# The front of a two-block transformer kernel: weights laid out by the host in one-transfer units, modulation columns by pairs of k-tiles, and a new order of norms, splits and decays

## The reference, cut to what matters

```
s_lat, s_ctx = silu(c), silu(c_ctx)
shift, scale, ... = split(s @ ada_w[i] + ada_b[i], 6)       # for latent and context
h = rms_norm(x) * (1 + scale) + shift                        # for x and for ctx
q, k, v, g = split(h @ ret_w_in)                             # retention, 4 heads; 1024 + 1024 + 2048 + 2048 columns
log_gamma = log_sigmoid(ret_decay_logit)                     # the decays of the retention masks
```

## Time and profile before

| | us |
|---|---|
| median of 3 runs | 2016.64 (2016.51 to 2016.98) |
| the profiled execution, its own time | 2016.68 |
| its span, first to last instruction | 2014.9 |
| TensorE busy in the span | 1981.0 |
| VectorE, ScalarE busy | 1323.6, 850.2 |
| mean granted TensorE clock | 0.997 of full |

### The profile page before, as it was taken

The page is one execution under the profiler, slowest core; times in us unless marked ns, Lnnn a source line. Parts: engine busy times, 40 slices in busy tenths (PEclk is TensorE's granted clock), DMA queues, the critical chain, the costliest instruction groups (busy, mean ns, idle before and its releaser), DMA issues.

```text
span 2014.9 us, 25505 instructions
## 1 busy us (share of the span) xinstructions
PE 1981.0 (98%) x10295; PEld 1650.7 (82%) x10295; DVE 1323.6 (66%) x1610; ACT 850.2 (42%) x1003; POOL 69.0 (3%) x122
## 2 busy tenths in 40 slices
PE   8999999999999999999999999999999999999998
PEld 6878778778888888877778888898888888988887
DVE  4887978556544354677676565766866577678565
ACT  4332332124222222446665553554544356545442
POOL 0000000000111001000000000000000000000000
PEclk9999999999999999999999999999999999999999
DMA  9644444243554243332136565544665555546552
GB/s 355 203 137 138 146 160 148 76 160 90 162 167 158 89 150 132 105 105 84 63 110 206 174 180 182 187 161 168 209 201 194 170 172 163 195 161 216 190 190 80
DMA packets 250807, 319.32 MB, mean 158 GB/s; under 512 B 10129, under 2 KB 166082, under 8 KB 250178
## 3 DMA queue, kind: packets, MB, share of 16 engines
q1 hardware_dynamic: 235152, 262.77, 40.4%
q0 software_dynamic: 14464, 53.27, 7.8%
q10 hardware_dynamic: 1074, 1.66, 0.2%
HBM read 316.61 MB, written 1.05 MB: 158 GB/s over the span
## 4 chain that ended last, share of the span: by engine, by line
PE 86%; DVE 6%; DVEq 2%; ACT 2%; DMA 1%; issue 1%; ACTq 1%; SPq 0%
PE ps L2325 13%; PE ps L2326 12%; PE ps L2320 6%; PE ps L2890 6%; PE ps L3151 6%; PE ps L2339 5%; PE ps L2335 5%; PE ps L2336 5%; PE ps L2807 3%; PE ps L2268 3%; PE ps L3154 3%; PE ps L2420 2%; PE ps L2896 2%; PE ps L2900 2%; PE ps L2897 2%; PE ps L2810 2%
## 5 line engine op out<-in xcount | busy, mean ns | idle before, releaser
L1244 DVE TENSOR_TENSOR w_lo<-raw,w_hi 128x2048 fp32r<-128x2048 f32 (+1 forms) x244 | 552.9, 2271 | 224.7 <-ACT w_hi L614 224.0
L614 ACT ACTIVATE w_hi<-raw 128x2048 fp32r<-128x2048 f32 (+1 forms) x244 | 462.0, 1898 | 291.5 <-PE ps L2320 185.9
L2325 PE MATMUL ps<-w_hi,big_hi 128*128 128x512 f32 x760 | 298.6, 393 | 0.8 <-DVE big_lo L1738 0.5
L2326 PE MATMUL ps<-w_hi,big_lo 128*128 128x512 f32 x760 | 296.1, 390 | 0.0
L2335 PE MATMUL ps<-hT_hi,w_hi 128*128 128x512 f32 (+1 forms) x512 | 192.2, 380 | 1.9 <-issue 1.0
L2336 PE MATMUL ps<-hT_lo,w_hi 128*128 128x512 f32 (+1 forms) x512 | 190.2, 376 | 0.0
L2325 PEld LDWEIGHTS ps<-w_hi,big_hi 128*128 128x128 f32 x760 | 142.8, 188 | 30.3 <-issue 1.0
L2326 PEld LDWEIGHTS ps<-w_hi,big_lo 128*128 128x128 f32 x760 | 142.8, 188 | 29.0 <-issue 0.5
L3151 PE MATMUL ps<-h_both,w_hi 128*128 128x512 f32 x512 | 127.9, 392 | 0.0
L1366 DVE SCALAR_TENSOR_TENSOR raw<-front,const,raw 128x512 f32<-128x512 f32 x168 | 118.8, 748 | 7.1 <-issue 1.3
L2339 PE MATMUL ps<-hT_hi,w_lo 128*128 128x512 f32 (+1 forms) x512 | 119.8, 376 | 0.6 <-DVE w_lo L1244 0.6
(11 more groups left out here) (320 smaller groups left out, 3151.1 us busy)
## 6 DMA issues: line engine op xcount, KB each, us to landing
raw<-ffn_w_in SPq DMA_DIRECT2D x88, 512.0 KB, 5.2
raw<-w_in SPq DMA_DIRECT2D x80, 512.0 KB, 4.6
raw<-w_up SPq DMA_DIRECT2D x64, 512.0 KB, 4.7
raw<-w_down SPq DMA_DIRECT2D x64, 512.0 KB, 4.5
raw<-ret_w_in SPq DMA_DIRECT2D x48, 512.0 KB, 5.4
front<-ada_w POOLq DMA_DIRECT2D x24, 1024.0 KB, 5.5
raw<-ffn_w_out SPq DMA_DIRECT2D x40, 512.0 KB, 4.3
raw<-ada_w POOLq DMA_DIRECT2D x64, 256.0 KB, 4.2
```

The source lines that it names most:

```text
L614: act.activation(SPLIT_HI[PAIR_OF[u]][:, 0:m], raw[:, RAW_OF[u], 0:m], ACT.Copy).then_inc(sem["hi_ready"], 1)
L1244: op(SPLIT_LO[PAIR_OF[u]][:, 0:m], raw[:, RAW_OF[u], 0:m], SPLIT_HI[PAIR_OF[u]][:, 0:m].bitcast(F32), ALU.subtract).then_inc(sem["lo_ready ...
L2325: pe.matmul(out, x[0][:, t * P:(t + 1) * P], w, start=start, stop=False)
L2326: pe.matmul(out, x[1][:, t * P:(t + 1) * P], w, start=False, stop=False)
```

## The change

- **Units.** The host lays every unit out as it stands in `raw` (`units`, 8 KiB per partition in one piece), in order of use, and SP issues one DMA for each. The matrices `ada_w` are laid out the same way (`ada`). The two-DMA code of SP is gone; the waits for `lo_ready` stay.
- **Modulation chunks.** Chunk j now has the shift and the scale columns of k-tiles 2j and 2j + 1 (256 + 256 columns), so that two k-tiles of both are complete after each chunk. ACT copies the sums (`row`), DVE's `mod_cols` makes two reductions and two additions and signals.
- **Shift and scale** of layer 0's first norm are applied by DVE (`modulated`: two operations on 256 columns, the split in high and low on 512), one k-tile at a time, latent and context together.
- **Columns** and the identity come in one DMA of ACT, already as columns; the transposes of the small vectors, their copies and the separate identity load are gone.
- **Orders.** SP: x, ctx, qa0, chunks 0, 1, 2, qb0, chunk 3, g00 and the rest. POOL fetches the tables after chunk 2 is summed, and its first pieces of further chunks after chunk 3. ACT: both norms, four turned tiles, then copies and splits in turn, g00's high part before head 0 begins. DVE: both norms, then `mod_cols`, `modulated` and the splits in turn, g00's low part and `decay_end` before head 0 begins. TensorE: qa0 and qb0 with 512 columns, a k-tile at a time, and more `awake` matmuls (128 columns, 24 at the start, 4 + 4 + 8 later).
- DVE's list for head 0 is otherwise the same, with one more wait, for the rotation tables.

The core of the diff (`weight_units`, not shown, yields the same slices in the same order as SP's old code; `modulation(2)` and `(3)` keep their places around `load(FIRST_END["qb0"])`):

```diff
-        const = sb("const", [P, C_HELD])
-        cols = sb("cols", [P, 161])
+        held = sb("held", [P, 161 + C_HELD])
+        cols, const = held[:, 0:161], held[:, 161:161 + C_HELD]
...
+            def load(n):
+
+                while s.loaded < n:
+                    u = s.loaded
+                    r, v, m = RAW_OF[u], RAW_BEFORE[u], SIZES[u]
+                    if v is not None:
+                        sp.wait_ge(sem["lo_ready"], v + 1)
+                    sp.dma_start(raw[:, r, 0:m], A["units"][u, :, 0:m]).then_inc(unit_in[r], 16)
+                    s.loaded += 1
...
+                for h in range(2):
+                    sp.dma_start(FRONT_IN[2 * j + h], A["ada"][j, :, 4 * h:4 * h + 4, :]).then_inc(front_in[2 * j + h], 16)
...
             sp.dma_start(X4[:, 0:2, :], token_rows(A["x"][0])).then_inc(sem["x_in"], 16)
+            sp.dma_start(X4[:, 2:4, :], token_rows(A["ctx"][0])).then_inc(sem["xc_in"], 16)
+            load(FIRST_END["qa0"])
             modulation(0)
-            sp.dma_start(FRONT_IN[3][:, 2:4, :], kpn(A["ada_w"][0])[:, 6:8, FRONT[1] * 512:(FRONT[1] + 1) * 512]).then_inc(front_in[3], 16)
-            part(w, 0, 0, RH * RDK)
+            modulation(1)
...
+            load(TOTAL_UNITS)
...
-            pool.wait_ge(front_in[3], 32)
-            fetch(X4[:, 2:4, :], token_rows(A["ctx"][0]), sem["xc_in"])
-            pool.wait_ge(sem["front_used"], 2)
             fetch(dec[:, 0, :], bcast(A["ret_decay_logit"].rearrange("a b c -> a (b c)"), 8), sem["dec_in"])
...
+            pool.wait_ge(sem["front_used"], 3)
+            fetch(const[:, C_DIST:C_SZ], A["table"][:, C_DIST:C_SZ], sem["const_in"])
+            fetch(const[:, C_RS:C_SEL], A["table"][:, C_RS:C_SEL], sem["rot_in"])
+            fetch(ROT_COS[1], A["table"][:, C_RK:C_RK + 256], sem["rot_in"])
             pool.wait_ge(sem["front_used"], 4)
-            fetch(const[:, C_DIST:C_SZ], A["table"][:, C_DIST:C_SZ], sem["const_in"])
-            fetch(const[:, C_RS:C_SEL], A["table"][:, C_RS:C_SEL], sem["const_in"])
-            pool.wait_ge(sem["mod_ready"], 4)
-            fetch(ROT_COS[1], A["table"][:, C_RK:C_RK + 256], sem["const_in"])
             for c in range(EARLY):
...
+            act.dma_start(held[:, 0:161 + P], A["columns"]).then_inc(sem["vec_in"], 16)
+            act.wait_ge(sem["vec_in"], 16)
...
+            first_squares(0)
+            first_root(0)
+            first_squares(1)
+            first_root(1)
+            for t in range(4):
+                turned_x(t)
+            row(0, 8192, 1)
             split(FIRST_END["qa0"])
-            act.drain()
-            act.wait_ge(sem["mod_ready"], 2)
-            modulate(0, 0, 1, 0, 0, lambda c: XTL[:, c, :])
-            first_norm(1)
             act.wait_ge(sem["dec_abs"], s.next("dec_abs"))
             act.activation(dec[:, 2, :], dec[:, 1, :], ACT.Exp, scale=-1.0).then_inc(sem["dec_exp"], 1)
-            turned_x(2)
-            turned_x(3)
+            row(1, 8704, 2)
+            row(0, 8192, 3)
+            split(FIRST_END["qb0"])
+            row(1, 8704, 4)
+            split(FIRST_END["g00"])
...
+            def mod_cols(b, j):
                 dve.wait_ge(sem["at_full"], s.next("at_full"))
+                for g in (0, 8):
+                    c = g + 2 * j
+                    m = mod[:, 0, c:c + 2, :]
+                    parts = bank(b)[:, 32 * g:32 * g + 256].rearrange("p (j q m) -> p j m q", j=2, q=4)[:, :, 0:2, :]
+                    dve.tensor_reduce(m, parts, AX.X, ALU.add)
+                drain()
+                for g in (0, 8):
+                    c = g + 2 * j
+                    m = mod[:, 0, c:c + 2, :]
+                    i = op(m, m, cols[:, c:c + 2].unsqueeze(2).to_broadcast([P, 2, 2]), ALU.add)
+                i.then_inc(sem["mod_ready"], 1)
+                drain()
...
+            def modulated(c):
+
+                xm = at(4096 + 512 * c, 2, 256)
+                for m, x in enumerate((XTL, XTC)):
+                    ts(xm[:, m, :], x[:, c, :], mod[:, 0, 8 + c, m:m + 1], mod[:, 0, c, m:m + 1], ALU.mult, ALU.add)
+                drain()
+                dve.tensor_copy(hT_hi[:, c, :], at(4096 + 512 * c, 512))
+                drain()
+                lo(hT_lo[:, c, :], at(4096 + 512 * c, 512), hT_hi[:, c, :]).then_inc(sem["h_part"], 1)
+
+            first_norm(0)
+            first_norm(1)
+            scaled_columns()
             dve.wait_ge(sem["dec_in"], s.next("dec_in", 16))
             dve.scalar_tensor_tensor(out=dec[:, 1, :], in0=x, scalar=-1.0, in1=x, op0=ALU.mult, op1=ALU.max).then_inc(sem["dec_abs"], 1)
-            first_norm(1)
+            dve.wait_ge(sem["xt_read"], 4)
+            mod_cols(2, 0)
+            modulated(0)
+            modulated(1)
+            split(FIRST_END["qa0"])
             decay_start()
             series(15, 13, 11, 9)
-            rows_split(1, 0)
-            row(0, 8960, 3)
-            row(1, 9472, 4)
-            mod_cols(2, 0, 1)
-            mod_cols(3, 0, 3)
+            mod_cols(3, 1)
+            modulated(2)
+            modulated(3)
+            mod_cols(2, 2)
+            modulated(4)
+            modulated(5)
+            split(FIRST_END["qb0"])
+            mod_cols(3, 3)
+            modulated(6)
+            modulated(7)
+            split(FIRST_END["g00"])
             decay_end()
-            rows_split(0, 4)
-            split(FIRST_END["qb0"])
-            rows_split(1, 4)
...
+            def first_high(name, k):
+                w = unit(name, 4)
+                pe.wait_ge(sem["h_part"], k + 1)
+                for j in range(4):
+                    out, js = bank(4 + j), slice(j * P, (j + 1) * P)
+                    pe.matmul(out, w[0][:, k % 4, js], hT(k)[0], start=(k == 0), stop=False)
+                    pe.matmul(out, w[0][:, k % 4, js], hT(k)[1], start=False, stop=False)
+
+            def first_low(name, k):
+                w = unit(name, 4)
+                lows(name)
+                for j in range(4):
+                    i = pe.matmul(bank(4 + j), w[1][:, k % 4, j * P:(j + 1) * P], hT(k)[0], start=False, stop=(k == KD - 1))
+                return i
+
+            pe.wait_ge(sem["ones_set"], 1)
+            awake(24)
+            pe.wait_ge(sem["vec_in"], 16)
             x_turned(0)
             x_turned(1)
-            half(0, 0, 1).then_inc(sem["front_used"], 1)
-            chunk(1, 1)
-            to_cols(2, 8960)
-            to_cols(3, 9472)
-            pe.wait_ge(sem["h_part"], 1)
-            features(4, "qa0", 0, (0, 1), 0, 256, True)
-            pe.wait_ge(sem["h_part"], 2)
-            features(4, "qa0", 0, (2,), 0, 256, False)
-            pe.wait_ge(sem["mod_ready"], 2)
+            awake(4)
             x_turned(2)
             x_turned(3)
-            features(4, "qa0", 0, (3,), 0, 256, False)
-            pe.wait_ge(sem["xt_read"], 4)
+            pe.wait_ge(sem["silu_c"], 1)
+            chunk(0, 0)
+            awake(4)
+            to_cols(2, 8192)
+            awake(8)
+            first_high("qa0", 0)
+            first_high("qa0", 1)
+            chunk(1, 1)
+            first_low("qa0", 0)
+            to_cols(3, 8704)
+            first_low("qa0", 1)
             chunk(2, 0)
+            first_high("qa0", 2)
+            to_cols(2, 8192)
+            first_high("qa0", 3)
+            first_low("qa0", 2)
+            used(first_low("qa0", 3))
             chunk(3, 1)
-            to_cols(2, 8960)
-            to_cols(3, 9472)
-            pe.wait_ge(sem["h_part"], 4)
-            features(4, "qa0", 0, (0, 1), 256, 256, False)
-            used(features(4, "qa0", 0, (2, 3), 256, 256, False))
-            pe.wait_ge(sem["h_part"], 6)
-            features(4, "qb0", 4, range(4), 0, 256, False)
-            pe.wait_ge(sem["h_part"], 8)
-            used(features(4, "qb0", 4, range(4), 256, 256, False))
+            first_high("qb0", 4)
+            to_cols(3, 8704)
+            first_high("qb0", 5)
+            first_low("qb0", 4)
+            first_low("qb0", 5)
+            first_high("qb0", 6)
+            first_high("qb0", 7)
+            first_low("qb0", 6)
+            used(first_low("qb0", 7))
...
+def laid_out(I):
+    import numpy as np
+    f = np.float32
+    units = np.zeros((TOTAL_UNITS, P, UNIT), f)
+    n = 0
+    for n, w in enumerate(weight_units(I)):
+        w = w.reshape(P, -1)
+        assert w.shape[1] == SIZES[n], (n, w.shape)
+        units[n, :, 0:w.shape[1]] = w
+    assert n + 1 == TOTAL_UNITS
+    w = [kpn(I["ada_w"][d]) for d in range(2)]
+    ada = [np.concatenate([w[0][:, :, c:c + 256] for c in (256 * j, D + 256 * j)], 2) for j in range(4)]
+    ada += [w[d][:, :, n * 512:(n + 1) * 512] for d, n in EXTRA]
+    rows = [I["ada_b"], I["c"], I["c_ctx"], I["ret_norm_g"], I["b_gate_2"], I["diff_subln_g"], np.eye(P, dtype=f)]
+    return {"units": units, "ada": np.ascontiguousarray(np.stack(ada)),
+            "columns": np.ascontiguousarray(np.concatenate([r.reshape(-1, P).T for r in rows], 1))}
```

(52 more changed lines are left out.)

265 lines of the change are left out of this document (110 added, 155 removed).

## The result

The changed kernel takes 2018.84 us (median of 20 runs, 2017.31 to 2024.24) against 2016.26 (20 runs, 2015.17 to 2017.23): a ratio of 1.0016 with an interval of 1.0009 to 1.0023. Predicted were 2013.8 and a range of 2011.0 to 2017.2. The kernel is slower by 2.6 us where I had forecast a gain of 2.8. It is within the 0.2% that I called no change, but the interval leaves zero out.

What follows compares the result with a forecast made beforehand. Head 0 was taken as bound by both TensorE and VectorE's list: TensorE, 5.9 us earlier, would wait for vb0's low part until 91.4 against 94.13. That gives 2.7, plus 0.1 rounding: 2016.64 - 2.8 = 2013.8 us, range 2011.0 to 2017.2.

Steps and rivals of the forecast that it cites:

- chunk 0's sums end at 17.4 + 1.1 = 18.5 ..., so the norms are hidden: Front: chunk 0 lands at 17.4, its second half takes 1.06 us; ACT's copies of x end by 18.0, so norms cost nothing.
- the clock falls in the front again: Rival, TensorE before 22.5 us: a fall to half clock loses 3.1 us, gain about 0, 2016.7 us; chance 0.10.
- 50.6 predicted: Start of head 0's list on VectorE, after g00's low part at 49.0 and `decay_end` of 1.6 us; before at 49.81.
- VectorE's list bounds head 0: Head 0: VectorE's unbroken rows from 49.81 to 93.45 leave 0.7 us margin, so an earlier TensorE alone gains nothing.
- 40.8: Length in us of VectorE's head 0 list to vb0's low part: 43.64 - 2.86, without g00's split and a 0.42 wait.
- 3.2 us of such waits: TensorE at head 0, arriving early, waits for low parts until 91.4; 0.3 of it for g10's.
- my 36 to 41: Landing time of chunk 3 in us, expected at 38.9; a landing outside this range would show the forecast wrong.
- Single-DMA units cost nothing: Units fetched by one DMA each, behind the front: costed at nothing, since the three slots hide them.
- no weight's transfer is waited for behind the front: The 1900 us left: none of TensorE's waits behind 60 us is for a DMA, so nothing changes there.
- The offset of +2.7 in place of -2.7: Start of vb0's first low matmul less 94.13, the kernel before's; forecast at 91.4, a gain of 2.7 us.
- The change does something else late: columns or norms later than 18.5: Rival, front: each us goes through to VectorE's list, slower from 2.8 us on, 2017 to 2021 us; chance 0.10.
- Slower than before: the wait that VectorE causes cools TensorE: Rival, ahead of vb0's low matmuls: a 3.2 us wait brings half clock, costing 3.1 us, 2016.9 us; chance 0.07.

Runs made afterwards that it cites:

- columns_vb: Changed kernel with the decays in the columns' transfer (no early fetch) and head 0's 32 high matmuls of vb0 before its first low one: 2013.35 us, ratio 0.9987.
- after: The changed kernel as first measured: median 2018.84 us, ratio 1.0016; its own profiled execution is the fastest of 20, 2017.31 us.
- dec_late: Changed kernel with POOL's fetch of the decays held back until ctx has landed: 2018.09 us, ratio 1.0009.
- dec_in_columns: Changed kernel with the decays as eight more host columns in the columns' transfer and no fetch by POOL: 2016.29 us, ratio 1.0004.
- dve_freed: Changed kernel with six of eight operations of VectorE's second weigh piece in head 0 left out: 2014.42 us, ratio 0.9992.
- units_only: Kernel before with only the units laid out by the host and fetched by one DMA each: 2015.77 us, ratio 0.9998.
- decays_early: Changed kernel with `decay_end` moved ahead of qb0's low part, into VectorE's wait for chunk 3: 2018.88 us, ratio 1.0011.
- awake_34: Changed kernel with `awake(24)` made `awake(34)`, 20 more filler matmuls before x is normed: 2019.16 us, ratio 1.0015.
- before_dec_early: Kernel before with only the fetch of the decays moved to the start of POOL's queue: 2017.66 us, ratio 1.0008.
- after_again: Changed kernel run again unaltered: 2018.18 us, ratio 1.0015; its profiled execution, 2018.71 us, is the one at the median.
- combined_early: Changed kernel with decays in the columns' transfer, vb0's high matmuls first, `awake(34)`, and `decay_end` ahead of qb0's low part: 2012.20 us, ratio 0.9979.
- combined: Changed kernel with decays in the columns' transfer, vb0's high matmuls first and `awake(34)`: 2013.06 us, ratio 0.9984.
- vb_high_first: Changed kernel with all 32 of head 0's high matmuls of vb0 ahead of its first low one: 2016.33 us, ratio 1.0002.

## Why the prediction was wrong

**The step that failed** is "chunk 0's sums end at 17.4 + 1.1 = 18.5 ..., so the norms are hidden". In the execution at the median it is 2.9 of the 5.2 us by which head 0's list is late; the rest are terms of the wrong size. The step rests on a cover, the landing of chunk 0. The profile after has 426 to 434 GB/s over these microseconds, so the cover was shorter than I had allowed: in columns_vb both halves of chunk 0 are summed without a wait from 15.93 on, so that the second had landed by 16.9; and in TensorE's order both pairs of turns stand ahead of both halves of chunk 0, so that 1.87 us of sums follow the norms and not 1.06. From then on the norms set the start of the front. I had written that without the cover their lateness counts fully. It did, and it had two sources that the sum didn't have:

- *The columns.* With the early fetch silu starts between 7.33 and 7.84 us in five profiled executions of the changed front, and at 6.23 in the sixth, that of after. Without the early fetch it starts at 6.27 to 6.47 in all five. I counted the fetch of the decays among the reordered small things and costed it at nothing. The experiment on the kernel before prices it: 1.7 us.
- *The clock.* In seven of the eight profiled executions of the changed front with 24 fillers, a wait of 2.6 to 4.4 us for x was followed by half clock; in the eighth, that of columns_vb, the wait was 2.0 and the clock stayed up. It cost 1.35 us by the pair above, and more in the execution at the median, where it was at half until 17.6: from the first turn to the last group of turns are 5.15 us there (12.47 to 17.62) and 2.88 in columns_vb. My rival "the clock falls in the front again" had it at 0.10, looked for it before 22.5, and took the gaps to be 1.5 to 2.5 us. They were longer in part because x was later, but not only: with the columns on time dec_late and dec_in_columns still wait 2.6 and 2.7 us, since the fillers end well before x is normed.

In numbers, for the execution at the median: start of the list 55.83 against 50.6 predicted, 5.2 us. Of this, 55.83 - 51.92 = 3.9 is norms by the comparison with columns_vb, which has neither source: the turns start 1.3 later (12.47 and 11.14; silu at 7.72 and not 6.40) and take 2.3 longer at half clock. These 3.6 are there when chunk 0 is summed (19.50 and 15.93). The other 1.3 are **terms of the right kind and the wrong size**. `modulated` takes 1.92 us a k-tile (21.25 to 23.17) where I had 1.6: its two operations on 256 columns take 0.81 to the cast and not 0.5, while the rest was read rightly; two of these k-tiles stand behind chunk 3's turn, 0.64. `decay_end` is 1.8 and not 1.6. TensorE lost 0.5 waiting for the third k-tile of h, where I had no wait. From the end of chunk 0's sums to the first matmul with h it is 4.5 us in after (18.9 to 23.4) and not 4.0, and the first two k-tiles take 3.9 and not 3.6. That makes 2.1; against it stands the end of chunk 0's sums at 17.8 in columns_vb, 0.7 before my 18.5. Set against the forecast itself, chunk 0's sums end 2.9 us late in this execution (21.4) and 0.4 in the fastest (18.9), and the list another 2.4 late in both. So even with the norms hidden the sizes would have left 0.4 of the 2.8 us of gain (an estimate, 2.8 - 2.4).

**What held.** VectorE's list bounds head 0 (dve_freed), with 40.9 us for 40.8. TensorE would reach vb0 early and wait for `w_lo`; 3.2 us of such waits were forecast, 0.3 of them at g10, and 4.0 measured, 1.5 of them at g10, since the list was later. Chunk 3's last half landed at 36.4, inside my 36 to 41. Single-DMA units cost nothing (units_only). But I had read that no weight's transfer is waited for behind the front from TensorE's waits alone; ScalarE does wait for units there, as shown below. The offset of +2.7 in place of -2.7 is 5.4 us, the 5.2 of the list and 0.2 of rounding, and the span of that execution is 2016.9, 2.0 over before's.

**The rivals.** "The change does something else late: columns or norms later than 18.5" is the one that came true, at 0.10; I had named the place and let the numbers of the cover decide against it. "The clock falls in the front again", also at 0.10, came true with it. "Slower than before: the wait that VectorE causes cools TensorE" is real too, but not in the profiled executions of after: it was seen in decays_early and awake_34, at 1.5 and 1.8 us and not 3.1. The Trainium skill, TensorE: Matmul & The Clock Gate, section HAM oscillation — how this bites in real kernels, has TensorE cooled by idle gaps longer than these. The traces differ: at vb0, waits of 2.5 us were followed by half clock in two of six, so the rule is no safe bound for this kernel.

**What stays open.** The range of after's runs, 7 us, is wider than before's 2, and none of those above 2019 has a trace. The traces show three things that differ from execution to execution. One is the columns and the clock in the front. Another is a fall of the clock near 1050 us, behind a wait of 1.8 us that both kernels have (windows of the first execution of after):

```profile
1048.00:1050.00 2.00, 2.00 (x11) 1.90 (x11) 1.33 (x5) 2.00 (x3) 0.00 (x0) 0.59 0.00 0
1050.00:1052.00 2.00, 2.00 (x12) 2.00 (x11) 1.53 (x1) 1.86 (x2) 0.00 (x0) 0.55 0.00 0
```

It is in ten of the fourteen profiled executions, units_only and before_dec_early with the old front among them, and not in before, after_again, dve_freed and combined_early. It need not cost anything: dec_late has it and is 2.2 us ahead of after_again in front of it and behind it. The third is a weight unit that lands late. ScalarE's rows at two places, of after and after_again, then of awake_34 and after_again:

```profile
1058.81 1.92 ACT L493 ACTIVATE w_hi<-raw 128x2048 fp32r<-128x2048 f32 x1 [2.32 <-DMA raw<-units]
1059.92 1.92 ACT L493 ACTIVATE w_hi<-raw 128x2048 fp32r<-128x2048 f32 x1 [1.09 <-DMA raw<-units]
```

```profile
1446.23 1.92 ACT L493 ACTIVATE w_hi<-raw 128x2048 fp32r<-128x2048 f32 x1 [3.19 <-DMA raw<-units]
1445.03 1.92 ACT L493 ACTIVATE w_hi<-raw 128x2048 fp32r<-128x2048 f32 x1 [1.65 <-DMA raw<-units]
```

At the first place after falls from 2.3 us ahead of after_again to 1.4; the long wait (2.2 to 2.6) is in six of the fourteen, before's among them, and the short one (1.1 to 1.7) in the others. At the second, awake_34 falls from 0.4 ahead to 0.8 behind; the wait is 2.8 to 3.4 there in it, combined and combined_early and 1.6 to 2.2 in the others. With one trace for each kernel neither can be tied to the change. Nor is it settled why the columns came at 6.23 once with the fetch in place.

## What to carry to other kernels

When a transfer gets faster, ask what it used to hide: the step behind it may now be set by small operations that were never on the path, here silu, squares and turns. A wait removed from a queue issues everything behind it earlier; price each of these DMAs at its new place, the smallest too. And do not only shorten the list that bounds a stage: give the waiting engine other work before it asks (vb_high_first), which takes the wait and its risk to the clock away together.

## What the runs showed of the hardware

- A broadcast of 8 floats to 128 partitions from POOL's queue, issued at 1.3 us, took 24 us of DMA engine time and halved what all transfers delivered from 6 to 8 us (164 and 133 GB/s against 357). In the kernel before the same fetch was issued at 19.51 behind that of ctx and landed 7.1 us later; its packets of 256 B took 0.02 us each there, and the windows from 24 to 28 us have 397 and 379 GB/s. The Trainium skill, DMA: Bandwidth & Descriptors, section Specifications, says that transfers reach line rate from 512 B up, and are read, modified and written below it. These packets are that small at both places, so it doesn't say why the place makes such a difference, and no run here shows that either.
- With rows of 8 KiB from the host's layout the front moved 418 to 434 GB/s in the windows from 8 to 32 us, the kernel before, with rows of 1 to 4 KiB for all but x and ctx, 347 to 415 in those from 4 to 42. The order and the number of the DMAs changed too, so the row length is the likely cause and not a shown one. The same page and section has one rate from 512 B up; here the measurement decides.
- Whether a wait of TensorE is followed by half clock isn't a matter of its length alone: 2.5 us went both ways at the same place in six executions, with 1.5 and 1.8 us lost in two and nothing in four.
